# The scale of the first norm as one row, spread by TensorE into PSUM, with zero products on TensorE ahead of the first tile

## The chip, the cores and the metric

One core of a Trainium2 chip runs the whole program. The metric is device time in microseconds (us), the median of a few executions. The engines are TensorE (PE, with its weight loads PEld), VectorE (DVE), ScalarE (ACT), GpSimd (POOL) and SyncE (SP). Each has a queue of its own that it works in order; semaphores tie the queues together. Transfers are issued from SP's and POOL's queues.

## The reference, cut to what matters

Two transformer blocks of two layers each run one after the other on 256 tokens of width 1024, all in float32. The change touches the very first step alone, the norm in front of the first layer's input projection:

```python
def rms_norm(x, g):
    xf = x.astype(jnp.float32)
    y = xf * lax.rsqrt(jnp.mean(xf * xf, axis=-1, keepdims=True) + NORM_EPS)
    return (y * g.astype(jnp.float32)).astype(x.dtype)

for l in range(DEPTH):                       # DEPTH = 2
    h = rms_norm(x, mix_norm_g[l])           # x: (1, 256, 1024), g: (1024,)
    proj = h @ w_in[l]                       # and so on: attention, mlp
```

## The kernel before

The 256 tokens are two tiles of 128 (x, one token per partition, 1024 elements each). The norm of a tile runs over four engines. ScalarE squares and sums (`norm_root`, L756) and takes the root (L759). VectorE takes the reciprocal (L682) and multiplies x by it and by the scale g, in two halves of 512 columns, into `xs` (`norm_vector`, L687). TensorE transposes `xs` in eight pieces of 128 columns into PSUM (`turn_bank`, L818, with the identity `ident`). ScalarE copies the transposes to a rounded high part `xT` (L771), and VectorE makes the low part, the difference (L777).

Products are made of high and low parts of both operands, three products each of the rounded kind (`crossed`, L449). The weights come from memory in pieces of 128x1024 (512 KB) through a ring of seven slots, issued from SP's queue (L382). ScalarE rounds a piece to `w_high` (L403), VectorE makes `w_low` (L406). Each engine's order is written out by hand. On VectorE the low part of the first piece stands between the scaled tile and the low parts of `xT`, three more behind those, and only then the reciprocal of the second tile. The first matrix of products (`gemm_first`, key `swq`) works six of the eight row blocks of the first tile, with three products each, before the transposes of the second tile.

The scale g is a row of 1024 numbers in memory. Before the change POOL's first transfer (`opening`, L1182) writes it to all 128 partitions of a page in SBUF, the second brings the second tile of x. SP's queue issues the first tile of x (L1177), `ident` (L1178), then the pieces of weights. TensorE's program begins with one wait for `ident`:

```python
    @block.tensor
    def _(pe):
        pe.wait_ge(c.flag("ident_in").sem, 16)
```

VectorE waits for the scale (`gain_in`) in front of its first reciprocal, together with the wait for the root (`norm_std`).

Of the kernel before, what the change touches and what calls it, by code (L numbers as in the profile page):

```python
# [5 lines left out]
F32 = mybir.dt.float32  # L6
# [6 lines left out]
P = 128  # L13
# [3 lines left out]
D = 1024  # L17
# [5 lines left out]
HALF = 512  # L23
# [42 lines left out]
class Stream:  # L66
# [3 lines left out]
    def __init__(self):  # L70
        self.blocks, self.at = [], {}
        self.widths, self.split = [], []
# [205 lines left out]
class Core:  # L278


    def __init__(self, nc, ctx, counts):
        self.rotated = None
        self.roots_tried = 0
        self.nc, self.ctx, self.counts, self.flags = nc, ctx, counts, {}

        def sb(name, shape, dtype=F32):
            return ctx.enter_context(nc.sbuf_tensor(name, shape, dtype))

        self.sb = sb
        self.psum = ctx.enter_context(nc.psum_tensor("psum", [P, 8, HALF], F32))  # L290
        self.x = sb("x", [P, NT, D])
        self.xs = sb("xs", [P, NT, D])

        self.xT = sb("xT", [P, KD, 2, SEQ], F32R)
        self.xT_high, self.xT_low = self.xT[:, :, 0, :], self.xT[:, :, 1, :]
        self.w_high = sb("w_high", [P, SPLITS, PIECE], F32R)


        room = SEQ * 4 * 32 + PAGES * 4096 + SLOTS * PIECE * 4
        first = nc.sbuf_base + -nc.sbuf_base % 32  # L300
        sb("stretch", [P, room // 4 + 8])

        def placed(name, shape, dtype, offset):
            return nc.alloc_sbuf_tensor_at(name, shape, dtype, offset=first + offset)

        self.wide = placed("gates", [P, 32, SEQ], F32, 0)
        self.arena = placed("pages", [P, PAGES, 1024], F32, SEQ * 4 * 32)
        self.rounded = placed("rounded_pages", [P, PAGES, 1024], F32R, SEQ * 4 * 32)
        self.hidden = {
            KF1: [placed(f"hidden_1_{i}", [P, KF1, SEQ], F32R, i * KF1 * SEQ * 4) for i in range(2)],  # L310
            KF2: [placed(f"hidden_2_{i}", [P, KF2, SEQ], F32R, i * KF2 * SEQ * 4) for i in range(2)],
        }
        self.ring = placed("ring", [P, SLOTS, PIECE], F32, SEQ * 4 * 32 + PAGES * 4096)
        self.w_low = placed("w_low", [P, SLOTS, PIECE], F32R, SEQ * 4 * 32 + PAGES * 4096)
        self.attn_p = sb("attn_p", [P, 2, HALF])
        self.attn_pT = sb("attn_pT", [P, 2, HALF])
        self.ident = sb("ident", [P, P])
        self.tails = sb("tails", [P, 2, P])
        self.identb = sb("identb", [P, P], BF16)
        self.masks = sb("masks", [P, 4, HALF], BF16)  # L320
        self.rope = sb("rope", [P, NT, 4, HD])
        self.stats = sb("stats", [P, NT, 2, 6])
        self.mv = sb("mv", [P, NT, 2])
        self.rstd = sb("rstd", [P, NT, 2])
        self.mx = sb("mx", [P, NT, 8])
        self.nmx = sb("nmx", [P, NT, 8])
        self.rsum = sb("rsum", [P, NT, 8])
        self.all_heads_sums = sb("all_heads_sums", [P, NT, 8])
        self.fac = sb("fac", [P, NT, 8])


        self.rows_1 = sb("rows_1", [P, DEPTH, 2 * HD + 8])
        self.cols_2 = sb("cols_2", [P, 53 + 12 + 64])

        self.rope_cmp = self.page(9)[0:16, 896:1024].rearrange("p (x d) -> p x d", x=2)
        self.vcmp = self.page(9)[0:16, 768:896]
        self.cmp_valid = sb("cmp_valid", [P, NT])
        self.idle = sb("idle", [P, 3])
        self.eps = sb("eps", [P, 3])
        self.kcmp = sb("kcmp", [P, P])  # L340
        self.kcmpT = sb("kcmpT", [P, 32])
        self.head_rows = sb("head_rows", [P, 8 + P])
        self.branch_gates = sb("branch_gates", [P, NT, 24])
# [828 lines left out]
def opening(c, io, block):  # L1172


    @block.sync
    def _(sp):
        sp.dma_start(c.x[:, 0, :], io["x_in"][:, 0, :]).then_inc(c.flag("x_in0").sem, 16)  # L1177
        sp.dma_start(c.ident[:, :], io["ident"]).then_inc(c.flag("ident_in").sem, 16)  # L1178

    @block.gpsimd  # L1180
    def _(pool):
        pool.dma_start(c.page(16), io["gains_1"][0:1, :].to_broadcast([P, D])).then_inc(c.flag("gain_in").sem, 16)  # L1182
        pool.dma_start(c.x[:, 1, :], io["x_in"][:, 1, :]).then_inc(c.flag("x_in1").sem, 16)
        c.wait_landed(pool, 1)
        pool.dma_start(c.rows_1[:, :, :].rearrange("p l w -> p (l w)"),
                       io["rows_1"].rearrange("(o l) w -> o (l w)", o=1).to_broadcast([P, DEPTH * (2 * HD + 8)])
                       ).then_inc(c.flag("params_1").sem, 16)
        pool.dma_start(c.rope[:, :, :, :], io["rope"]).then_inc(c.flag("rope_in").sem, 16)
        pool.dma_start(c.tails[:, :, :], io["tails"]).then_inc(c.flag("tails_in").sem, 16)
        pool.dma_start(c.masks[:, :, :], io["masks"]).then_inc(c.flag("masks_in").sem, 16)  # L1190
        pool.dma_start(c.identb[:, :], io["ident"]).then_inc(c.flag("masks_in").sem, 16)
        pool.wait_ge(c.flag("idle_set").sem, 1)

    @block.vector
    def _(dve):
        dve.memset(c.idle[:, :], 0.0).then_inc(c.flag("idle_set").sem, 1)
        for i, eps in enumerate((RMS_EPS, LN_EPS, 4 * LN_EPS)):
            dve.memset(c.eps[:, i:i + 1], eps).then_inc(c.flag("eps_set").sem, 1)


def block_1(c, io, block, stream):
# [41 lines left out]
    gain = c.page(16)  # L1243
# [12 lines left out]
    def added(t, n):  # L1256
        _, b, use = banks.groups["down", t, n]
        return c.flag(f"drained{b}").at(DEPTH - 1, use + 1)

    @block.tensor  # L1260
    def _(pe):
# [15 lines left out]
        for l in c.layers(1):  # L1277
            def turn(j, t, l=l):
                return lambda h: c.norm_turn(pe, l, j, t, h, c.xs)

            if l == 0:
                for h in range(2):
                    turn(0, 0)(h)
            c.turn_later = turn(0, 1)
# [8 lines left out]
            def logits(h):  # L1293
                heads = [(c.psum[:, 4 + x % 2, :], slice(HD * (x % 2), HD * (x % 2 + 1)), x // 2) for x in (h, h + 1)]
                if h == 0:
                    if l == 0:
                        pe.wait_ge(c.flag("masks_in").sem, 32)
                        pe.wait_ge(c.flag("tails_in").sem, 16)
                    for key in ("sbq", "sbk"):
                        for n in range(2):  # L1300
                            c.wait_drained(pe, l, banks, (key, n))
                if h >= 2:
                    pe.wait_ge(*c.flag("sb_weighed").at(l, h))
                for z, _, _ in heads:
                    pe.matmul(z[:, 0:P], c.identb[:, :], c.masks[:, 3, 0:P], start=True, stop=False,
                              skip_group_check=True)
                    pe.matmul(z[:, SEQ:SEQ + P], c.identb[:, :], c.masks[:, 3, 0:P], start=False, stop=False,
                              skip_group_check=True)
                for z, r, k in heads:
                    pe.matmul(z[:, 0:SEQ], sbkT[r, k, 0:P], sbqT[r, k, :], start=False, stop=True,  # L1310
                              skip_group_check=True)
                for z, r, k in heads:
                    pe.matmul(z[:, SEQ:SEQ + P], sbkT[r, k, P:SEQ], sbqT[r, k, P:SEQ], start=False,
                              stop=True, skip_group_check=True).then_inc(*c.flag("sb_logits").one())
# [239 lines left out]
    def _(dve):  # L1554
# [6 lines left out]
        def add(key, layer, t, n):  # L1561
            half = c.x[:, t, n * HALF:(n + 1) * HALF]
            dve.tensor_tensor(half, half, c.filled(dve, layer, banks, (key, t, n)), ALU.add
                              ).then_inc(*c.drained(banks, (key, t, n)))
            c.wait_drained(dve, layer, banks, (key, t, n))

        for l in c.layers(1):
# [6 lines left out]
            def window_heads():  # L1574
# [20 lines left out]
                for i, (src, width, heads, ss, gain) in enumerate(((swq, 512, 8, c.rsum, 0), (swkv, P, 2, c.fac, HD))):  # L1595
# [10 lines left out]
                    for t in range(NT):  # L1606
# [2 lines left out]
                                 tmp[:, 2, 0:width], tmp[:, 3, 0:width], "roped" if t == NT - 1 else None)  # L1609
                        yield  # L1610

            c.norm_vector(dve, l, 0, c.x, c.xs,
                          first_rows if l == 0 else lambda t, n: add("down", l - 1, t, n), gain, None, split, -1,
                          lambda: dve.wait_ge(*c.flag("gain_in").at(l, 16)))
            side = window_heads()
            for key in ("swq", "swkv"):
                after(key)
# [1462 lines left out]
```

## Time and profile before

| | us |
|---|---|
| median of 3 runs | 2228.23 (2225.65 to 2231.48) |
| profiled execution | 2233.68 |
| its span in the profile | 2231.9 |
| TensorE busy | 2207.0 |
| VectorE busy | 1552.2 |
| ScalarE busy | 1110.0 |
| GpSimd busy | 198.4 |

The span is the part of the profiled execution that the trace covers, from the first instruction on. The times of the rows count from the span's start. A row of the timeline merges several instructions where they follow one another; "xcount" says how many. What stands in square brackets is the idle time of the engine in front of the row and what ended it.

### The profile page before, as it was taken

How to read it: one execution, taken by the hardware profiler on the slowest of the kernel's cores; microseconds unless marked ns; L12 is line 12 of the kernel's file. 1: busy time of each engine (PE TensorE's matmuls, PEld its weight loads, DVE VectorE, ACT ScalarE, POOL GpSimd, SP SyncE). 2: the span in 40 equal slices, each digit the busy share in tenths (PEclk: the TensorE clock that was granted, in tenths of full speed). 3: DMA queues.
4: the chain of work that ended last, by engine and by line, in shares of the span. 5: the costliest groups of instructions: out<-in, count | busy, mean ns of one | idle time of the engine just before them, and what ended most of it. 6: DMA issues, size and time to landing. Idle time of an engine off the chain costs nothing.

```text
span 2231.9 us, 34104 instructions
## 1 busy us (share of the span) xinstructions
PE 2207.0 (99%) x13650; PEld 1900.3 (85%) x13662; DVE 1552.2 (70%) x2163; ACT 1110.0 (50%) x1719; POOL 198.4 (9%) x191
## 2 busy tenths in 40 slices
PE   8999999999999999999999999999999999999998
PEld 7888888888888888888889988888888888998887
DVE  5777845677864775777787677567666777777764
ACT  4745434655543544445454554455444546355443
POOL 0010200001200110000004011011100000310110
PEclk9999999999999999999999999999999999999999
DMA  7445565445555755554535465565556444355553
GB/s 238 142 142 180 188 200 186 152 133 180 182 193 187 243 189 189 185 182 152 171 105 171 169 215 184 193 236 192 190 184 193 161 164 138 133 199 181 187 189 133
DMA packets 109245, 397.72 MB, mean 178 GB/s; under 512 B 12384, under 2 KB 12528, under 8 KB 108832
## 3 DMA queue, kind: packets, MB, share of 16 engines
q1 hardware_dynamic: 104256, 377.01, 50.8%
q0 software_dynamic: 4832, 18.53, 2.6%
q8 instruction: 109, 1.79, 0.3%
q14 instruction: 48, 0.39, 0.0%
HBM read 395.00 MB, written 1.05 MB: 177 GB/s over the span
## 4 chain that ended last, share of the span: by engine, by line
PE 96%; DVE 2%; ACT 1%; DMA 1%; issue 0%; DVEq 0%; SPq 0%; ACTq 0%; POOLq 0%
PE psum L449 44%; PE psum L600 29%; PE psum L599 15%; PE psum L818 2%; PE psum L963 2%; PE psum L940 1%; PE psum L927 1%; PE psum L898 1%; PE psum L2043 1%; PE psum L1319 0%; DMA ring<-in_weights 0%; DMA pages<-in_gains 0%; PE psum L1333 0%; ACT attn_p L1103 0%; DVE xs L2396 0%
## 5 line engine op out<-in xcount | busy, mean ns | idle before, releaser
L406 DVE TENSOR_TENSOR w_low<-ring,w_high 128x1024 fp32r<-128x1024 f32 x704 | 858.5, 1231 | 332.7 <-ACT w_high L403 331.3
L403 ACT ACTIVATE w_high<-ring 128x1024 fp32r<-128x1024 f32 x704 | 734.6, 1056 | 511.2 <-DMA ring<-in_weights 506.1
L600 PE MATMUL psum<-xT,w_high 128*128 128x512 f32 x2784 | 983.0, 397 | 0.0
L599 PE MATMUL psum<-xT,w_low 128*128 128x256 f32 x2784 | 790.3, 284 | 0.0
L600 PEld LDWEIGHTS psum<-xT,w_high 128*128 128x128 f32 x2784 | 522.8, 188 | 123.5 <-issue 1.0
L599 PEld LDWEIGHTS psum<-xT,w_low 128*128 128x128 f32 x2784 | 526.1, 189 | 3.9 <-issue 1.4
L449 PE MATMUL psum<-w_high,hidden 128*128 128x512 f32 x1216 | 376.9, 390 | 0.0
L449 PEld LDWEIGHTS psum<-w_high,hidden 128*128 128x128 f32 x1216 | 228.3, 188 | 47.2
L449 PE MATMUL psum<-w_low,hidden 128*128 128x512 f32 x608 | 236.6, 389 | 0.0
L449 PE MATMUL psum<-w_high,xT 128*128 128x512 f32 (+2 forms) x640 | 193.3, 382 | 0.7 <-DVE xT L777 0.6
L449 PE MATMUL psum<-rounded_pages,w_high 128*128 128x256 f32 x896 | 165.6, 286 | 0.0
L620 POOL TENSOR_TENSOR hidden<-attn_pT,hidden 128x256 fp32r<-128x256 f32 (+1 forms) x108 | 110.0, 1019 | 575.2 <-ACT hidden L2158 383.5
L449 PEld LDWEIGHTS psum<-rounded_pages,w_high 128*128 128x128 f32 x896 | 139.4, 191 | 1.8
L449 PEld LDWEIGHTS psum<-w_high,xT 128*128 128x128 f32 x640 | 118.3, 189 | 23.0 <-issue 2.0
L449 PEld LDWEIGHTS psum<-w_low,hidden 128*128 128x128 f32 x608 | 114.1, 188 | 23.7
L609 DVE TENSOR_REDUCE attn_p<-psum 128x256 f32<-128x512 f32 x136 | 93.8, 689 | 57.2 <-PE psum L600 57.0
L449 PE MATMUL psum<-rounded_pages,w_low 128*128 128x256 f32 x448 | 126.7, 283 | 0.0
L1103 ACT ACTIVATE attn_p<-psum,nmx 128x256 f32<-128x256 f32 (+2 forms) x176 | 67.9, 399 | 118.1 <-DVE nmx L1052 91.1
L449 PE MATMUL psum<-w_high,rounded_pages 128*128 128x512 f32 x384 | 123.7, 395 | 0.0
L449 PE MATMUL psum<-w_low,xT 128*128 128x512 f32 (+2 forms) x320 | 117.9, 379 | 0.0
L609 DVE TENSOR_REDUCE attn_pT<-psum 128x256 f32<-128x512 f32 x80 | 55.2, 690 | 63.8 <-PE psum L600 63.8
L2171 ACT ACTIVATE attn_p<-attn_p 128x256 f32<-128x256 f32 x80 | 33.4, 418 | 128.9 <-DVE attn_p L609 128.9
(238 smaller groups left out, 2089.0 us busy)
## 6 DMA issues: line engine op xcount, KB each, us to landing
ring<-in_weights SPq DMA_DIRECT2D x706, 512.0 KB, 3.5
pages<-in_affine POOLq DMA_DIRECT2D x16, 512.0 KB, 5.5
ring<-in_weights SPq DMA_DIRECT2D x8, 440.0 KB, 3.2
pages<-in_gains POOLq DMA_DIRECT2D x4, 512.0 KB, 4.8
pages<-in_mem POOLq DMA_DIRECT2D x2, 1024.0 KB, 6.6
pages<-in_bias POOLq DMA_DIRECT2D x2, 988.0 KB, 11.8
ring<-in_weights SPq DMA_DIRECT2D x4, 384.0 KB, 3.2
pages<-in_rows POOLq DMA_DIRECT2D x2, 512.0 KB, 5.8
```

Source lines behind the costliest of these rows:

```text
L403: eng.activation(high, raw, ACT.Copy).then_inc(self.flag("w_rounded").sem, 1)
L406: eng.tensor_tensor(self.w_low[:, piece % SLOTS, 0:width], raw, high.bitcast(F32), ALU.subtract).then_inc(self.flag("w_split").sem, 1)
L449: m = pe.matmul(out, a, b, start=(first and i == 0), stop=(last and i == len(pairs) - 1))
L599: pe.matmul(out[:, 0:SEQ], low, self.xT_high[:, k, :], start=(k == 0), stop=False, skip_group_check=True)
L600: m = pe.matmul(out, high, self.xT[:, k, :, :].rearrange("p x s -> p (x s)"), start=False, stop=(k == kn - 1), skip_group_check=True)
L609: dve.tensor_reduce(out, h.rearrange("p (x s) -> p s x", x=2), AX, ALU.add).then_inc(*self.drained(banks, key))
L620: pool.tensor_tensor(low, whole[:, n % (4 // tiles), :], high.bitcast(F32), ALU.subtract).then_inc(*self.flag("hidden").one())
L818: m = pe.transpose(out, src, self.ident[0:n, 0:n])
L898: m = pe.matmul(bank[:, i * w:(i + 1) * w], q, k, start=not started, stop=True, skip_group_check=True)
L963: m = pe.matmul(self.psum[rows, 7, h * dv:(h + 1) * dv], self.attn_pT[0:n, u % 2, c * P + rows.start:c * P + rows.stop], a["v"](h, kt), st ...
L1103: m = act.activation(self.attn_p[:, u % 2, i * w:(i + 1) * w], self.psum[:, 4 + u % 2, i * w:(i + 1) * w], ACT.Exp, bias=self.nmx[:, t, h: ...
L2171: act.activation(silu[:, n % 4, :], silu[:, n % 4, :], ACT.Silu).then_inc(*c.flag("silu").one())
```

## The change

The scale's transfer brings one row of 4 KB to one partition instead of 128 copies. VectorE first fills 512 columns of `xT` with zeros and a row `ones` with ones. TensorE multiplies the zeros five times (512 columns each, rounded kind), then waits for the row and multiplies `ones` by it, once for each half, in plain float32, so that PSUM banks 2 and 3 hold the scale on all 128 partitions; then it multiplies zeros four times more. VectorE reads the scale of the first layer's first norm from those banks, for both tiles; its first reciprocal waits for the two spreading products. All other norms stay as they were. The wait for `ident` stays at the head of TensorE's program.

```diff
+        self.ones = sb("ones", [1, P])
...
     @block.gpsimd
     def _(pool):
-        pool.dma_start(c.page(16), io["gains_1"][0:1, :].to_broadcast([P, D])).then_inc(c.flag("gain_in").sem, 16)
+        pool.dma_start(c.page(16)[0:1, :], io["gains_1"][0:1, :]).then_inc(c.flag("gain_in").sem, 16)
         pool.dma_start(c.x[:, 1, :], io["x_in"][:, 1, :]).then_inc(c.flag("x_in1").sem, 16)
...
     @block.vector
     def _(dve):
+        dve.memset(c.xT[:, 0, :, :].bitcast(F32), 0.0).then_inc(c.flag("warm_set").sem, 1)
+        dve.memset(c.ones[:, :], 1.0).then_inc(c.flag("ones_set").sem, 1)
         dve.memset(c.idle[:, :], 0.0).then_inc(c.flag("idle_set").sem, 1)
...
             if l == 0:
+                idle_columns = c.xT[:, 0, :, :].rearrange("p x s -> p (x s)")
+
+                def warm(n):
+                    for _ in range(n):
+                        pe.matmul(c.psum[:, 0, :], idle_columns[:, 0:P], idle_columns, start=True, stop=True)
+
+                pe.wait_ge(c.flag("warm_set").sem, 1)
+                warm(5)
+                pe.wait_ge(c.flag("ones_set").sem, 1)
+                pe.wait_ge(*c.flag("gain_in").at(l, 16))
+                for n in range(2):
+                    pe.matmul(c.psum[:, 2 + n, :], c.ones[:, :], gain[0:1, n * HALF:(n + 1) * HALF], start=True, stop=True
+                              ).then_inc(c.flag("gain_spread").sem, 1)
+                warm(4)
                 for h in range(2):
                     turn(0, 0)(h)
...
-            c.norm_vector(dve, l, 0, c.x, c.xs,
-                          first_rows if l == 0 else lambda t, n: add("down", l - 1, t, n), gain, None, split, -1,
-                          lambda: dve.wait_ge(*c.flag("gain_in").at(l, 16)))
+            if l == 0:
+                c.norm_vector(dve, l, 0, c.x, c.xs, first_rows, c.psum[:, 2:4, :].rearrange("p n w -> p (n w)"), None,
+                              split, -1, lambda: dve.wait_ge(c.flag("gain_spread").sem, 2))
+            else:
+                c.norm_vector(dve, l, 0, c.x, c.xs, lambda t, n: add("down", l - 1, t, n), gain, None, split, -1,
+                              lambda: dve.wait_ge(*c.flag("gain_in").at(l, 16)))
```

The head of TensorE's order before (the names in brackets are the flags that a row waits for; `xn_ready` is a finished half of `xs`):

```order
L1260 UNCONDITIONAL_BRANCH [waits barrier_Pool_Activation_PE_DVE_SP_release]
L818 MATMUL psum<-ident,xs 128x128 [waits xn_ready,ident_in]
L818 MATMUL psum<-ident,xs 128x128 x3
L818 MATMUL psum<-ident,xs 128x128 [waits xn_ready]
L818 MATMUL psum<-ident,xs 128x128 x3
L449 MATMUL psum<-w_high,xT 128x512 [waits w_split,turned_dve,drained0]
```

And in the changed kernel, where line numbers are shifted (L819 is the old L818; `pages,ones` is the spreading of the scale):

```order
L1263 UNCONDITIONAL_BRANCH [waits barrier_Pool_Activation_PE_DVE_SP_release]
L1289 MATMUL psum<-xT 128x512 [waits warm_set,ident_in]
L1289 MATMUL psum<-xT 128x512 x4
L1296 MATMUL psum<-pages,ones 128x512 [waits gain_in,ones_set]
L1296 MATMUL psum<-pages,ones 128x512
L1289 MATMUL psum<-xT 128x512 x4
L819 MATMUL psum<-ident,xs 128x128 [waits xn_ready]
```

Eleven products stand ahead of the first transpose, and the wait for `ident` moved from the transpose to the first of them.

The head of VectorE's order before, from its first instruction to the second half of `xs`:

```order
L1196 MEMSET idle 128x3
L1198 MEMSET eps 128x1 x3
L1553 UNCONDITIONAL_BRANCH
L682 RECIPROCAL rstd<-rstd 128x1 [waits norm_std,gain_in,x_in0]
L687 SCALAR_TENSOR_TENSOR xs<-x,rstd,pages 128x512 [waits dve_step]
L687 SCALAR_TENSOR_TENSOR xs<-x,rstd,pages 128x512
```

And in the changed kernel:

```order
L1197 MEMSET xT 128x512
L1198 MEMSET ones 1x128
L1199 MEMSET idle 128x3
L1201 MEMSET eps 128x1 x3
L1570 UNCONDITIONAL_BRANCH
L683 RECIPROCAL rstd<-rstd 128x1 [waits norm_std,gain_spread,x_in0]
L688 SCALAR_TENSOR_TENSOR xs<-x,rstd,psum 128x512 [waits dve_step]
```

Two fills are put in front, and the reciprocal waits for TensorE's `gain_spread` where it waited for the transfer `gain_in`.

## Rows read from the trace of the kernel before

**Rows 1.** The page's head: the span, and each engine's busy time.
```profile
span 2231.9 us, 34104 instructions
PE 2207.0 (99%) x13650; PEld 1900.3 (85%) x13662; DVE 1552.2 (70%) x2163; ACT 1110.0 (50%) x1719; POOL 198.4 (9%) x191
```

**Rows 2.** Busy time by stretch: length, PE, PEld, DVE, ACT, POOL, PEclk, DMA share, GB/s.
```profile
0.00:20.00 20.00, 9.91 (x40) 8.05 (x41) 9.78 (x17) 10.27 (x16) 4.11 (x11) 1.00 0.89 311
20.00:500.00 480.00, 479.56 (x3148) 414.92 (x3153) 330.08 (x457) 250.33 (x372) 27.03 (x21) 1.00 0.52 168
```

**Rows 3.** TensorE's waits: who for whom, us in total, times, longest.
```profile
PE psum L818 <- DVE xs L687: 9.5, 1, 9.5
```

**Rows 4.** Timeline to 12 us: start, length, engine, line, operation.
```profile
1.24 0.42 SPq L1178 DMA_DIRECT2D ident<-in_ident  x1
1.32 0.69 POOL L1182 DMA_DIRECT2D pages<-in_gains  x1 [0.81 <-POOLq L3071]
...
6.41 0.29 ACT L759 ACTIVATE rstd<-mv,eps 128x1 f32<-128x1 f32 x1
8.38 0.16 DVE L682 RECIPROCAL rstd<-rstd 128x1 f32<-128x1 f32 x1 [7.36 <-DMA pages<-in_gains]
8.58 1.41 DVE L687 SCALAR_TENSOR_TENSOR xs<-x,rstd,pages 128x512 f32<-128x512 f32 x2
...
9.48 1.94 PE L818 MATMUL psum<-ident,xs 128*128 128x128 f32 x8 [9.48 <-DVE xs L687]
9.91 1.22 DVE L406 TENSOR_TENSOR w_low<-ring,w_high 128x1024 fp32r<-128x1024 f32 x1
...
11.23 0.69 DVE L777 TENSOR_TENSOR xT<-psum,xT 128x512 fp32r<-128x512 f32 x1
```

**Rows 5.** Transfers: count, KB, median us from issue to landing (last: whole program).
```profile
pages<-in_gains POOLq DMA_DIRECT2D x1, 512.0 KB, 7.0
...
ident<-in_ident SPq DMA_DIRECT2D x1, 64.0 KB, 4.1
identb<-in_ident POOLq DMA_DIRECT2D x1, 32.0 KB, 9.0
...
ring<-in_weights SPq DMA_DIRECT2D x706, 512.0 KB, 3.5
```

**Rows 6.** Timeline of TensorE, 12 to 20 us.
```profile
12.03 0.76 PE L449 MATMUL psum<-w_high,xT 128*128 128x512 f32 x1 [0.60 <-DVE xT L777]
12.59 0.63 PE L449 MATMUL psum<-w_low,xT 128*128 128x512 f32 x1
13.02 1.05 PE L449 MATMUL psum<-w_high,xT 128*128 128x512 f32 x2
...
15.15 0.53 PE L449 MATMUL psum<-w_low,xT 128*128 128x512 f32 x1
15.52 0.62 PE L449 MATMUL psum<-w_high,xT 128*128 128x512 f32 x2
15.97 0.40 PE L449 MATMUL psum<-w_low,xT 128*128 128x512 f32 x1
...
18.27 0.60 PE L818 MATMUL psum<-ident,xs 128*128 128x128 f32 x4
```

**Rows 7.** Timeline of TensorE near 69 us: plain float32 products, two records each.
```profile
69.44 0.81 PE L1319 MATMUL psum<-pages,tails 128*128 128x384 f32 x2
70.08 0.38 PE L1321 MATMUL psum<-pages,tails 128*128 128x128 f32 x2
```

**Rows 8.** Timeline of VectorE, 13 to 17 us.
```profile
13.03 3.50 DVE L406 TENSOR_TENSOR w_low<-ring,w_high 128x1024 fp32r<-128x1024 f32 x3 [0.18 <-ACT w_high L403]
16.64 0.17 DVE L682 RECIPROCAL rstd<-rstd 128x1 f32<-128x1 f32 x1
```

**Rows 9.** VectorE by line and form: count, busy us, mean ns, idle before.
```profile
L2396 DVE SCALAR_TENSOR_TENSOR xs<-x,psum 128x512 f32<-128x512 f32 x32 | 21.9, 683 | 14.7 <-PE psum L449 14.2
L687 DVE SCALAR_TENSOR_TENSOR xs<-x,rstd,pages 128x512 f32<-128x512 f32 x16 | 11.3, 749 | 0.3
```

## The prediction

> **What bounds the kernel now.** I read the first lines of the page first. TensorE is busy for 2207.0 of 2231.9 us [rows 1], so all its idle time together is 24.9 us, and a change that leaves TensorE's own work alone can give back no more than a part of that. The view of busy time by stretch says where the idle time lies: TensorE works 9.91 of the first 20 us, so 10.1 us are lost there, and from 20 to 500 us it loses 0.44 us [rows 2]. The view of waits names the largest one: 9.5 us, once, for the first scaled tile `xs` of VectorE [rows 3]. The change sits in exactly this stretch. Behind it TensorE runs without a gap, so whatever moment it reaches its steady stream is carried unchanged to the end: a microsecond lost or won at the start is a microsecond of the total, and nothing multiplies it. That alone limits the effect to a few tenths of a per cent.
>
> The timeline of the first 13 us gives the chain [rows 4]. ScalarE has the root of the mean of squares done at 6.41 + 0.29 = 6.70. VectorE starts its reciprocal only at 8.38: it waits for the scale `gains`, issued at 1.32 and 7.0 us in flight [rows 4, 5], so it landed at 8.32. From 8.38 (call this moment T0) VectorE works without a gap: the reciprocal and two halves of `xs`, then the first low weight part from 9.91, then at 11.23 the first `xT` part, 0.69 long; TensorE's first product follows at 12.03, that is T0 + 3.65.
>
> The rows of TensorE after that show its clock [rows 6]. Products of 512 columns start 0.43 us apart (12.59 to 13.02), and after 15.52 they start 0.23 apart (15.52 to 15.97, two of them): 512 columns in 0.43 are 1.2 GHz, in 0.23 nearly 2.4 GHz. (The column of the granted clock says 1.00 for the whole stretch [rows 2], so the level is read from the starts.) The rise lies between 15.15 and 15.52, say 15.3: 5.8 us after TensorE's first work (the transposes at 9.48), 3.3 us after the first 512-column product.
>
> **The change part by part.** *What it hopes to remove* is the gap from 6.70 to 8.38 on VectorE, 1.7 us, and the slow products after 12.03. But VectorE now waits for TensorE, and TensorE's queue is in order: in the order of TensorE the five zero products stand ahead of the two spreading ones, and the first of the five carries the wait for `ident`, which used to stand at the first transpose and was covered by the wait for `xs`. `ident` is issued at 1.24 and is 4.1 us in flight [rows 4, 5]: it lands at 5.34. The gains took 0.06 from landing to the reciprocal, so TensorE starts at 5.40, not near 1.
>
> *Five zero products* at the slow 0.43: 2.15, to 7.55.
>
> *The two spreading products* are plain float32, not the rounded kind of the weight products. A float32 product of 384 columns is two records, and the pair takes 70.08 - 69.44 = 0.64 us at the full clock [rows 7]: 0.32 per 384 columns, twice the time per column of a 512-column weight product. For 512 columns that is 0.64 x 512/384 = 0.85 per product, 1.71 for both at the full clock and 3.41 at the half one. That only one of 128 rows is filled takes nothing off in this sum: no row shows that fewer rows are quicker.
>
> *When does the clock rise?* Counted from the first 512-column product as before, at 5.40 + 3.3 = 8.7; counted from the first work, at 5.40 + 5.8 = 11.2. TensorE's first work is now a run of 512-column products, so I take the row that is nearest, 3.3 us. Then the spreading runs slow from 7.55 to 8.7, 1.15 of 3.41 or 34%, and the other 66% of 1.71 take 1.13: 9.83. With 0.2 for the last product's way out and the signal (the pair of 384 columns lasts 0.81 where its successor starts after 0.64 [rows 7]), the reciprocal starts at 10.0: T0 moves by +1.6. With the late rise: 7.55 + 3.41 + 0.2 = 11.2, +2.8.
>
> *What comes back behind T0.* The four later zero products fit between the spreading and the first transpose, which comes 1.1 us after T0 as before (9.48 - 8.38): four take 0.92 at the full clock. To the first `xT` part nothing changes, since VectorE is busy all the way. From then on both engines gain. The second half's transposes take half the time (four of them last 0.60 us at 18.27 against 1.94 for eight at 9.48), so the next high parts and the three low parts, which VectorE works from 13.03 to 16.53 [rows 8], each about 0.4 to 0.5 us sooner after T0. TensorE's eight slow products, 0.2 too long each, cost 1.6 us; at full speed six products of one piece of weights take 1.38 and VectorE delivers a low part every 1.17, so TensorE has to wait some 0.5 for the second piece. What is left is about 1.0 us: the transposes of the second tile, at 18.27 or T0 + 9.9 before, come at about T0 + 8.9, behind a second reciprocal at T0 + 7.8 instead of T0 + 8.26.
>
> *The small parts.* Filling 512 columns of `xT` with zeros is not in the trace; at most 0.75 us by VectorE's operations of that width, and more than nothing ([rows 9] has 0.683 and 0.749 with two inputs, this has none). It ends before 2 us, while TensorE waits for `ident` until 5.34, and the `eps` filled behind it are needed for the root at 6.41: covered, and without the cover at most 0.75. The scale as a PSUM operand: an operation of the same kind and width with a PSUM input takes 0.683 against 0.749 with all in SBUF [rows 9], so four of them win 0.26 at most, of which one or two lie on the chain: -0.1, which I leave in the bounds. The Trainium skill ("VectorE: DVE Perf Modes", section on the TRN2 errata) has a fixed part of 58 cycles for SBUF to SBUF and of 120 for PSUM to SBUF; by it each would take 0.06 longer and the sum would be +0.1, an estimate; the trace's rows say the opposite, and the sum goes by them.
>
> *The row's landing.* POOL's queue issues 4 KB where it issued 512 KB. TensorE needs it at 7.55. Bounds: it lands no later than the 512 KB did, 8.32, if it is like its predecessor; the trace has also a 32 KB transfer of the same queue that took 9.0 us (`identb`, behind 512 KB of masks [rows 5]), which would be 10.3. At the other end, the 512 KB pieces of weights take 3.5 us at the median [rows 5]: 4.8. It is the first transfer of its queue, as the gains were, and those had 128 times as much to move, so I take a landing before 7.55 and no wait. The Trainium skill ("DMA: Bandwidth & Descriptors", Anatomy of one DMA) gives a transfer from this queue about 2 us and its bytes over 436 GB/s: by that it lands near 3.4, an estimate, and the sum is the same; `identb`'s 9.0 us show that this trace does not bear the rule out under load. The 508 KB that no longer flow make the second tile of x and the weights land earlier; ScalarE and VectorE reach them later than before, so nothing comes of it.
>
> *Sum*: +1.6 for T0, -1.0 behind it: +0.6 us. In the profiled execution's own time that is 2233.68 + 0.6; that execution lies above all three timed runs (2225.65 to 2231.48), so I carry the difference to their median: 2228.23 + 0.6 = 2228.8 us.
>
> **The rivals.** *The spread is early, faster.* With less traffic beside it `ident` may land after 3.5 us as a piece of weights does: 4.74. If the clock were full from the start, TensorE would run 1.15 + 1.71 from 4.8, and T0 would be 7.9: -0.5, and with the 1.0 behind it -1.5: 2226.7. For it: the gains' half megabyte was in flight at the same time as x and `ident`. Against: the second tile of x follows on the same queue at once, and no row shows TensorE at full clock in its first 3 us.
>
> *Half clock throughout.* If the zeros and the thin products do not raise the clock, T0 is 11.2, the four later zeros end 0.6 after the transposes could start, and nothing comes back: +3.4, 2231.6. Against: the rise before came within 5.8 us of any work. If it only comes at 11.2, the rest is at full clock and the sum is +2.8 - 1.0 = +1.8, 2230.0.
>
> *Slower: the row is late and blocks TensorE.* The second wait of TensorE stands in front of the spreading, the later zeros and all transposes, so nothing passes it. It decides from a landing after 7.55. With `identb`'s 9.0 us: 10.3, then the spreading slow again after 2.8 us of idleness, 13.7, T0 = 13.9, +5.5, and less than 1.0 back: about +5, 2233. To be slower by 0.3% (6.7 us) the row would have to land after 11 us.
>
> *The change does nothing to T0*: the spreading happens to end at 8.2. This needs `ident` 1.6 us earlier than before; -1.0, 2227.2. It lies inside the first rival.
>
> **How the numbers follow.** Forecast, a spread between 9.4 and 11.2 and a sum from 0 to +1.8: 0.70. Early spread: 0.12. Half clock throughout: 0.08. Late row: 0.07. Something outside these: 0.03. No case but the last and the tail of the late row leaves the 0.3% (6.7 us, about what a measurement of this kernel can tell from no change): faster 0.02, same 0.95, slower 0.03. The range joins the mechanisms' -1.5 to +3.4 with the scatter of a few runs (the three lie 5.8 us apart): 2225.4 to 2232.8.
>
> **What would show it.** In the profile after: TensorE's first work at about 5.4, not at 1 to 2; five products 0.43 apart; four float32 records whose spacing falls from 0.85 to 0.43; the reciprocal at about 10.0, released by TensorE and not by a transfer; TensorE's first weight product 3.6 after it and from there 0.23 apart with a wait for a low part after the sixth; transposes of the second tile near 18.9. TensorE's busy time grows, and its idle time falls by about as much, with the span unmoved. I am wrong if the reciprocal starts before 8.4, if TensorE waits for the row after the fifth zero product, or if any difference arises behind 20 us.

## The result, and the profile after

The changed kernel takes 2231.26 us (median of 20 runs, 2230.05 to 2233.91); beside it the kernel before took 2226.72 (20 runs). The ratio is 1.0018, 95% interval 1.0012 to 1.0025, so the change costs 2.7 to 5.6 us. The forecast was +0.6: 2228.8 for a median of 2228.23. It stays within the 0.3% (6.7 us) that the prediction named, and it is slower by more than the measurement's scatter.

The page's head of the changed kernel: TensorE is busy for 2.6 us more than in [rows 1], with its extra products.

```profile
span 2229.6 us, 34145 instructions
PE 2209.6 (99%) x13675; PEld 1900.8 (85%) x13675; DVE 1551.1 (70%) x2165; ACT 1108.8 (50%) x1719; POOL 199.2 (9%) x191
```

(The spans of the two profiled executions, 2231.9 and 2229.6, are one execution each and lie the other way round than the medians: the one of before was above every one of its first three timed runs. What is compared below is the start, stage by stage, and the times of many runs.)

The timeline of TensorE in the changed kernel, for [rows 4, 6]: start, length, operation, count, and the wait in front.

```profile
5.67 2.50 PE L1289 MATMUL psum<-xT 128*128 128x512 f32 x5 [5.67 <-DMA ident<-in_ident]
8.10 3.78 PE L1296 MATMUL psum<-pages,ones 1*128 1x512 f32 x4
11.81 2.08 PE L1289 MATMUL psum<-xT 128*128 128x512 f32 x4
13.68 1.56 PE L819 MATMUL psum<-ident,xs 128*128 128x128 f32 x8
16.20 0.47 PE L450 MATMUL psum<-w_high,xT 128*128 128x512 f32 x1 [0.95 <-issue]
16.50 0.40 PE L450 MATMUL psum<-w_low,xT 128*128 128x512 f32 x1
16.74 0.63 PE L450 MATMUL psum<-w_high,xT 128*128 128x512 f32 x2
...
18.14 0.50 PE L450 MATMUL psum<-w_high,xT 128*128 128x512 f32 x1 [0.31 <-DVE w_low L407]
...
22.82 0.47 PE L450 MATMUL psum<-w_high,xT 128*128 128x512 f32 x1
```

The reader is to see three things. TensorE starts only when `ident` lands. The four records of the spreading take 3.7 us, from 8.10 to 11.81, 0.93 each in the mean, and the four zero products behind them are still slow: 1.87 us to 13.68, 0.47 each. And from 16.20 on the weight products run at the full rate (16.50 to 16.74). The last row is the first product behind both turns of the second tile; I call it the stream's start, since TensorE is busy without a gap from there. It stood at 19.64 before, so the start is 3.18 us later:

```profile
19.64 0.47 PE L449 MATMUL psum<-w_high,xT 128*128 128x512 f32 x1
```

The timeline of VectorE there, for [rows 4, 8]:

```profile
0.98 0.48 DVE L1197 MEMSET xT<- 128x512 f32 x1 [0.98 <-PEq L3091]
...
11.98 0.16 DVE L683 RECIPROCAL rstd<-rstd 128x1 f32<-128x1 f32 x1 [10.35 <-PE psum L1296]
...
15.40 1.29 DVE L778 TENSOR_TENSOR xT<-psum,xT 128x512 fp32r<-128x512 f32 x2 [0.69 <-ACT xT L772]
```

The reciprocal comes at 11.98 instead of 8.38, released by TensorE. VectorE then waits 0.69 us for the high part, since the transposes began 1.70 after the reciprocal instead of 1.10: the slow zeros stood in front of them.

The transfers, for [rows 5]:

```profile
ident<-in_ident SPq DMA_DIRECT2D x1, 64.0 KB, 4.4
...
pages<-in_gains POOLq DMA_DIRECT2D x1, 4.0 KB, 4.5
```

The row lands at 1.32 + 4.5 = 5.8, long before TensorE asks for it.

### The profile page after: what moved, and what is told of

The parts are those of the page before. It is cut to its first block, busy times and chain, and to the rows that moved or that the text cites. A ratio compares the mean times of both kernels' runs of the same rounds, so it can differ in the third digit from the quotient of the medians.

```text
span 2229.6 us, 34145 instructions
## 1 busy us (share of the span) xinstructions
PE 2209.6 (99%) x13675; PEld 1900.8 (85%) x13675; DVE 1551.1 (70%) x2165; ACT 1108.8 (50%) x1719; POOL 199.2 (9%) x191
## 4 chain that ended last, share of the span: by engine, by line
PE 96%; DVE 2%; ACT 1%; issue 0%; DMA 0%; DVEq 0%; SPq 0%; ACTq 0%
PE psum L450 43%; PE psum L601 28%; PE psum L600 15%; PE psum L819 2%; PE psum L964 2%; PE psum L941 1%; PE psum L899 1%; PE psum L928 1%; PE psum L2063 1%; PE psum L1336 0%; DVE w_low L407 0%; ACT attn_p L1104 0%; ACT psum L753 0%; PE psum L1350 0%; DVE x L688 0%
```

## The experiments

The theory after the result (A): products of zeros do raise TensorE's clock, but in the changed kernel the run of spreading products, one row high, keeps it at the half level, 1.2 GHz; so spreading and later zeros are slow, and everything hangs on them. The rivals: zeros don't raise it at all (B); or the rise was late by chance (C). "Stream" is the first product behind the second tile's turns, as above; 19.64 before, 22.82 in the change.

| run | reciprocal | stream | ratio to before, 95% |
|---|---|---|---|
| the change | 11.98 | 22.82 | 1.0018 (1.0012 to 1.0025) |
| e8, the change again | 11.86 | 23.08 | 1.0022 (1.0014 to 1.0031) |
| e1, zeros alone | 8.03 | 19.71 | 1.0000 (0.9992 to 1.0009) |
| e2, no zeros | 9.79 | 21.59 | 1.0009 (1.0000 to 1.0018) |
| e3, ident later | 9.69 | 20.86 | 1.0011 (1.0002 to 1.0020) |
| e4, rounded spread | 9.38 | 21.84 | 1.0012 (1.0004 to 1.0021) |
| e5, x behind the scale | 8.00 | 24.87 | 1.0024 (1.0014 to 1.0035) |
| e6, zeros to the products | 7.88 | 23.68 | 1.0018 (1.0010 to 1.0027) |
| e7, full rows, zeros | 7.46 | 20.66 | one run, 2227.93 us |
| e12, one row, zeros | 7.32 | 23.61 | 1.0024 (1.0015 to 1.0034) |
| e10, spread in full rows | 12.56 | 22.47 | 1.0012 (1.0003 to 1.0020) |
| e9, halves and early | 7.20 | 22.28 | 1.0004 (0.9996 to 1.0013) |
| e11, halves, plain order | 7.05 | 18.11 | 1.0003 (0.9992 to 1.0013) |

Reciprocal and stream are read from one profiled execution of each kernel. In all twelve rows with an interval the shift of the stream against 19.64 lies within the interval of the time (the change: 3.18 in 2.7 to 5.6; e9: 2.64 in -0.9 to +2.9). That agrees with a start that is carried to the end; the intervals, some 3 to 5 us wide, prove no more.

### Zeros alone

```diff
-pool.dma_start(c.page(16)[0:1, :], io["gains_1"][0:1, :])       # against the change
+pool.dma_start(c.page(16), io["gains_1"][0:1, :].to_broadcast([P, D]))
...
-pe.matmul(c.psum[:, 2 + n, :], c.ones[:, :], gain[0:1, ...])    # and VectorE waits for gain_in again
-warm(4)
+warm(3)
```

> The scale comes by the old transfer of 512 KB and VectorE waits for that; only the zero products (eight, behind the wait for ident) are left of the change. Theory A (zero products raise TensorE's clock; what kept it at the half level for 9 us in the changed kernel is the run of one-row float32 products between them): the reciprocal stays at 8.4, the starts of the products fall from 0.43 to 0.23 us apart between 8.5 and 9.5, the first weight products run at the full rate, and the steady stream behind the second tile's transposes begins about 1.0 us earlier than before (19.64): ratio 0.9995. Theory B (products of zeros don't raise the clock, whatever stands between them): weight products 0.43 apart until about 15 as before, stream at 19.6, ratio 1.000.

TensorE in this run:

```profile
5.34 3.54 PE L1289 MATMUL psum<-xT 128*128 128x512 f32 x8 [5.34 <-DMA ident<-in_ident]
...
8.48 0.40 PE L1289 MATMUL psum<-xT 128*128 128x512 f32 x1
9.03 1.32 PE L819 MATMUL psum<-ident,xs 128*128 128x128 f32 x8 [0.15 <-DVE xs L688]
12.32 0.76 PE L450 MATMUL psum<-w_high,xT 128*128 128x512 f32 x1 [1.97 <-DVE xT L778]
12.88 0.63 PE L450 MATMUL psum<-w_low,xT 128*128 128x512 f32 x1
```

The last zero product lasts 0.40 where the slow ones of [rows 6] last 0.63, and the eight transposes take 1.32 where they took 1.94: zeros raised the clock, 3.1 us after they began. B falls. But TensorE then stood for 1.97 us until the first weight product, and that started slow again, 0.43 apart. So the zeros gave nothing back here, neither in the stream nor in the time. The expected -1.0 missed: A had the rise right and forgot the gap behind the transposes.

### No zeros; ident later; the change again

```diff
-pe.wait_ge(c.flag("warm_set").sem, 1)      # e2: and no fill of xT
-warm(5)
...
-warm(4)
```

> The change without any zero product and without their fill: the spreading products follow the landing of ident and of the row. Both theories: spreading from about 5.9 (row 5.8, ident 5.7), four records 0.93 apart, the reciprocal at 9.8 instead of 11.98, transposes not held up; the clock rises only behind the first weight products at 13.4, so near 16.5; stream at 21.0, +1.4 us against before and 1.8 to 3 less than the change: ratio 1.0006. A third theory C (any work raises the clock, it was only late by chance): spacing of the four records falls before the last, reciprocal at 9.0, stream at about 19.0, ratio 0.9998.

```diff
 def _(pe):                                  # e3
-    pe.wait_ge(c.flag("ident_in").sem, 16)
...
     warm(4)
+    pe.wait_ge(c.flag("ident_in").sem, 16)
     for h in range(2):
         turn(0, 0)(h)
```

> The change with the wait for ident moved from the head of TensorE's program to the first transpose. Five zero products from 1.6 to 3.8, then TensorE idle until the row lands at 5.8, spreading to 9.6, reciprocal at 9.8 (2.2 earlier than in the change), four zero products to 11.4. Theory A: the zeros from 9.6 on raise the clock at 12 to 13, during or just behind the transposes, stream at 20.3, +0.6 against before. Theory B: the transposes wait for slow zeros until 11.4, the first weight products come at 13.9 and are slow until 15 or later; stream at 21.3, +1.6.

> The changed kernel once more, for a second look at when its clock rises. Theory A (the one-row products don't raise it): spreading records 0.93 apart all four, reciprocal near 12.0, rise at 13 to 16. If the late rise was chance: rise between 8.5 and 11, reciprocal at 10 to 11. Ratio 1.001 to 1.002 by theory A.

Without zeros the reciprocal was at 9.79, as expected, and the stream at 21.59, 0.6 later than expected: the clock rose only at 18.1, not near 16.5.

```profile
5.94 3.75 PE L1293 MATMUL psum<-pages,ones 1*128 1x512 f32 x4 [5.94 <-DMA pages<-in_gains]
```

The spreading begins at 5.94 there and at 8.10 in the change: the five zeros in front cost it 2.2 us, and that is the difference of the reciprocals. In the run with `ident` later TensorE shows:

```profile
5.84 3.75 PE L1295 MATMUL psum<-pages,ones 1*128 1x512 f32 x4 [1.82 <-DMA pages<-in_gains]
9.52 2.08 PE L1288 MATMUL psum<-xT 128*128 128x512 f32 x4
11.39 1.88 PE L819 MATMUL psum<-ident,xs 128*128 128x128 f32 x8
13.90 0.47 PE L450 MATMUL psum<-w_high,xT 128*128 128x512 f32 x1 [0.64 <-issue]
```

Zeros and transposes behind the spreading are slow, the weight products at 13.90 fast: the rise comes after 12.5, more than 3 us after the last zeros began. The stream, 20.86, lies between A's 20.3 and B's 21.3. The second profile of the change (e8) gave nearly the first one's numbers: four records in 3.71, reciprocal 11.86, all eight transposes slow until 15.3, where in the first the clock rose within them, at 14.6. C has no support.

### Is it float32, the single row, or its data?

```diff
-self.ones = sb("ones", [1, P])              # e4
+self.ones = sb("ones", [1, P], F32R)
...
-pool.dma_start(c.page(16)[0:1, :], io["gains_1"][0:1, :])
+pool.dma_start(c.rounded[0:1, 16, :], io["gains_1"][0:1, :])
```

> The change with the row and the ones of the rounded kind of the weight products, so that each spreading product is one record instead of two slower ones; the row is rounded by its transfer, so the scale loses its last digits. Order and zeros as in the change. Both theories: spreading in 0.86 instead of 3.7 us, reciprocal at 9.2. Theory A: clock full by about 9.5, stream at 19.4, -0.2 against before. If it is the single row of data and not the float32 kind that fails to raise the clock, 10 to 12 and stream at 19.9. Theory B: later zeros to 10.7 hold the transposes by 0.4, weight products slow until 14 to 16, stream at 20.9, +1.2.

```diff
-pe.matmul(c.psum[:, 2 + n, :], c.ones[:, :], gain[0:1, n * HALF:(n + 1) * HALF], start=True, stop=True
+pe.matmul(c.psum[:, 2 + n, :], idle_columns[:, 0:P].bitcast(F32), idle_columns.bitcast(F32), start=True,      # e7
+pe.matmul(c.psum[:, 2 + n, :], idle_columns[0:1, 0:P].bitcast(F32), idle_columns[0:1, :].bitcast(F32), ...    # e12
```

> The changed kernel's order of products, with the two spreading products replaced by two float32 products of the same columns whose 128 rows are all filled (zeros by zeros); the scale comes by the old transfer. If it is the single filled row that left the clock at the half level: full rate 3 to 4 us after the first zero product, so at 8.5 to 9.5, spacing of the float32 records from 0.85 to 0.43, all zeros done by 11.0. If float32 products of any height do it: records 0.85 to 0.93 apart to the end, zeros 0.43 apart until after 13, as in the changed kernel.

> The twin of e7_full_rows: the same order and the same transfer of the scale, the two float32 products of zeros one row high instead of 128. Nothing else differs, the data neither. In e7_full_rows the four zero products behind them ran at the full rate, 0.23 apart from 11.3 on, 5.9 us after the first zero product. If the single row is what kept the clock down in the changed kernel: the four float32 records 0.93 apart, the four zeros behind them 0.43 to 0.47 apart, rise 2.8 to 4.5 us after these began, so at 14 to 16. If it was the data of the row, or chance: zeros 0.23 apart from about 11.5 on as in the twin.

Rounded products of one row, e4:

```profile
8.07 1.22 PE L1296 MATMUL psum<-rounded_pages,ones 1*128 1x512 f32 x2
9.22 2.08 PE L1289 MATMUL psum<-xT 128*128 128x512 f32 x4
...
18.01 0.53 PE L450 MATMUL psum<-w_low,xT 128*128 128x512 f32 x1
```

The spreading shrinks to 1.15 us and the reciprocal to 9.38, but the clock stays half until 18.1, so a late rise does not need the float32 kind. (e4 leaves out the exactness of the scale: its output is a tenth off, and it stands for its timing alone.) By itself e4 does not show that the single row is the cause: its products ahead of the transposes cover 5.5 us (5.64 to 11.09), and in e6, further down, zeros of 128 rows alone took 5.6 us to raise the clock. The twins e7 and e12 differ by the height of two products of zeros alone. TensorE with 128 rows, and then with one:

```profile
7.65 3.59 PE L1294 MATMUL psum<-xT 128*128 128x512 f32 x4
8.50 1.06 PE L1294 MATMUL psum<-xT 128*128 128x512 f32 x1
...
11.31 0.62 PE L1289 MATMUL psum<-xT 128*128 128x512 f32 x2
11.54 0.62 PE L1289 MATMUL psum<-xT 128*128 128x512 f32 x2
...
11.99 1.04 PE L819 MATMUL psum<-ident,xs 128*128 128x128 f32 x8
14.05 0.47 PE L450 MATMUL psum<-w_high,xT 128*128 128x512 f32 x1 [1.02 <-issue]
```

```profile
7.67 3.78 PE L1294 MATMUL psum<-xT 1*128 1x512 f32 x4
11.38 2.08 PE L1289 MATMUL psum<-xT 128*128 128x512 f32 x4
13.25 1.91 PE L819 MATMUL psum<-ident,xs 128*128 128x128 f32 x8
...
19.32 0.78 PE L450 MATMUL psum<-w_high,xT 128*128 128x512 f32 x2
```

(The row at 8.50 is one of the four records above it, the rows at 11.31 and 11.54 share a record: they come from narrow windows.) With 128 rows the zeros behind start 0.23 apart (11.31 to 11.54), the transposes take 1.04, and the stream begins at 20.66. With one row the zeros take 0.47 each, the transposes 1.91, and the full rate comes only after 19.3; the stream begins at 23.61, 2.95 us later, and the time is that of the change. The data are the same, so for what stands behind the two products it is the single row. One profile stands for each twin, but others agree: with one-row products in between, 8.0 us of work up to the transposes did not raise the clock in e12 (5.24 to 13.25), in the change or in e8, while with 128 rows and no wait in between the rise came within 5.7 us in every run with zeros. Two sizes missed: even with 128 rows the four float32 records stayed slow (7.65 to 8.50 is 0.85, as between one-row records), so the rise came only near 11, 5.7 us after the first zero product, against 3.1 in the run with zeros alone; and with one row it came not at 14 to 16 but past 19.3. So the single row does not explain why the spreading itself is slow in the change; it explains that the clock is still half behind it.

### The spreading in full rows

```diff
-self.ones = sb("ones", [1, P])
+self.ones = sb("ones", [P, P])              # ones in row 0, zeros below; page 16 filled with zeros first
...
-... gain[0:1, n * HALF:(n + 1) * HALF], start=True, stop=True
+... gain[:, n * HALF:(n + 1) * HALF], start=True, stop=True
```

> The changed kernel with the spreading products made 128 rows high: ones is a 128x128 tile with ones in its first row and zeros below, and the page that takes the row is filled with zeros first, so that the same scale comes out. The row's transfer waits for the fills, issued near 2.8, landing near 7.2, still ahead of the fifth zero. If the one filled row is what kept the clock down: rise 3 to 4 us after the first zero at 5.6, so at 8.6 to 9.6, spread by 10.0 to 10.7, reciprocal at 10.2 to 10.9 instead of 11.9, later zeros at the full rate, stream at 20.5 to 21.2 against 22.8 to 23.1 of the change. If not: reciprocal at 11.9 and stream at 22.9.

```profile
8.88 3.58 PE L1301 MATMUL psum<-pages,ones 128*128 128x512 f32 x4 [0.74 <-DMA pages<-in_gains]
...
12.53 0.63 PE L1293 MATMUL psum<-xT 128*128 128x512 f32 x2
12.77 0.63 PE L1293 MATMUL psum<-xT 128*128 128x512 f32 x2
```

The row landed at 8.8 and not at 7.2, so TensorE waited and the reciprocal came later, at 12.56, against the expected 10.2 to 10.9. The clock behaves as in e7: the spreading is slow with full rows too, 3.68 us from its start to the reciprocal against 3.88 in the change, so the expected rise within it did not come. The zeros behind it start 0.24 apart (12.53 to 12.77) where they start 0.43 or more apart in the change. The stream, 22.47, misses the expected 20.5 to 21.2 but gains 0.35 on the change in spite of the later reciprocal: it comes 9.91 us behind it, against 10.84 in the change.

### Can a version beat both?

```diff
 pool.dma_start(c.page(16), io["gains_1"][0:1, :].to_broadcast([P, D])).then_inc(...)
+pool.wait_ge(c.flag("gain_in").sem, 16)     # e5, and e6 with zeros from 1.5 us and behind the transposes
 pool.dma_start(c.x[:, 1, :], io["x_in"][:, 1, :]).then_inc(...)
```

> The kernel before with one wait more: POOL issues the second tile of x only when the 512 KB of the scale have landed. No zeros, no spreading. If the scale's 7.0 us come from sharing its queue with the second tile of x: landing near 6.5, reciprocal at 6.9 instead of 8.4, first weight product at 10.6, stream at 18.3, -1.3 us: ratio 0.9994. If the weights' pieces are what it shares with: landing and reciprocal stay at 8.0 to 8.4, ratio 1.000; and if the first piece of weights then lands late the low part of it holds VectorE, 1.000 too. The slower end: the second tile of x comes after 15 and its sum of squares is late, +0.5.

> The run before this one (e5_x_behind_scale), with zero products around the first transposes: eighteen from 1.5 us on, ahead of the wait for ident, and five more between the transposes and the first weight product (zeros in a slot of w_high that is written later). Theory A: clock full by 5 to 6, kept to the first weight product, which starts at 10.6 and runs 0.23 apart at once; stream at 17.3, 1.0 before the run without zeros: ratio 0.999. If the clock falls in the gaps that stay: as the run without zeros, or up to 0.5 later because the last five zeros are slow.

Without the second tile of x behind it the scale landed 6.6 us after its issue. With the tile behind it it took 7.0 (before), 6.6 (e1), 6.1 (e7) and 5.9 (e12), so no gain from the wait is shown. And the tile then came too late, by the row of VectorE in e5:

```profile
15.63 0.69 DVE L777 TENSOR_TENSOR xT<-psum,xT 128x512 fp32r<-128x512 f32 x1 [4.09 <-DMA x<-in_x_in]
```

VectorE stands for 4.09 us at a wait for the second tile that lies in front of the first tile's second half: 5.2 us for the stream, 3.1 to 7.8 in time. e6 falls with it, though its zeros kept the clock up to the first weight products: transposes in 1.23, first weight products 0.23 apart. The rise came later than the hoped 5 to 6; TensorE in e6, with two of the eighteen zeros alone:

```profile
1.52 6.90 PE L1289 MATMUL psum<-w_high 128*128 128x512 f32 x18 [1.52 <-DVE w_high L1198]
6.38 0.63 PE L1289 MATMUL psum<-w_high 128*128 128x512 f32 x1
7.12 0.40 PE L1289 MATMUL psum<-w_high 128*128 128x512 f32 x1
```

```diff
-lambda: dve.wait_ge(c.flag("gain_spread").sem, 2))                    # e9, e11: first half waits for 1, second for 2
+lambda: dve.wait_ge(c.flag("gain_spread").sem, 1), half_way=half_way)
...
-warm(5)                                     # zeros in a slot of w_high, from 1.5 us, ident waited for later
+warm(10)
...
-warm(4)
+warm(2)                                     # and behind them the wait for ident
...
+                warm(3)                     # behind the transposes; 6 in e11
```

> The row spread as in the change, with three edits: zeros start at 1.5 (ident waited for only at the first transpose, ten products, in a slot of w_high that is written later), VectorE waits for each half of the spread scale on its own with the first low weight part between them, and three more zeros stand between the transposes and the first weight product. By the theory that zeros raise the clock and one-row products don't: clock full somewhere between 4.6 and 7 us. If it is full when the row lands at 5.8: first half spread by 6.9, reciprocal at 7.1, first weight product at 10.8, stream at 18.0, -1.6 against before: ratio 0.9993. If it is still at the half level there: first half by 7.9, second by 9.8, first weight product near 11.6, stream at 19.0 to 19.3, -0.4 to -0.6. Rival: the row or the order of VectorE costs more than that (low weight part waits for its piece), +0.5.

> The run e9_halves_and_early with VectorE's old order restored (the first low weight part behind both halves of the scaled tile, each half waiting for its own spreading product) and six instead of three zeros between the transposes and the first weight product. What the earlier runs say adds up to: clock full before 5, spreading from 5.9 in 1.9 to 2.0, reciprocal at 7.2, second half done by 8.9; then the first low weight part waits for the first piece of weights, which ScalarE took up at 6.9 to 9.4 in the other runs. Taken up at 7: first weight product at 11.0, at the full rate, stream at 18.1, -1.5. Taken up at 9.4: first weight product at 12.6, stream at 19.7, 0. So between ratio 0.9993 and 1.000; the theory that it is the single filled row that keeps the clock down would be wrong if the rate fell back within the spreading.

In both the zeros from 1.5 us had raised the clock before the row landed, and the spreading ran at the full rate. TensorE in e9, then TensorE and VectorE in e11:

```profile
5.98 1.95 PE L1297 MATMUL psum<-pages,ones 1*128 1x512 f32 x4 [0.48 <-DMA pages<-in_gains]
7.86 1.12 PE L1290 MATMUL psum<-w_high 128*128 128x512 f32 x2
8.78 1.05 PE L821 MATMUL psum<-ident,xs 128*128 128x128 f32 x4
```

```profile
5.83 1.98 PE L1297 MATMUL psum<-pages,ones 1*128 1x512 f32 x4
...
9.37 2.91 PE L1290 MATMUL psum<-w_high 128*128 128x512 f32 x6
12.07 0.50 PE L450 MATMUL psum<-w_high,xT 128*128 128x512 f32 x1
...
18.11 0.47 PE L450 MATMUL psum<-w_high,xT 128*128 128x512 f32 x1
```

```profile
7.05 0.16 DVE L683 RECIPROCAL rstd<-rstd 128x1 f32<-128x1 f32 x1 [5.42 <-PE psum L1297]
```

Four records in 1.98 us, the reciprocal at 7.05, 1.3 before that of the kernel before, and a stream at 18.11, 1.5 earlier. But the clock fell again behind the one-row products: in e9 at once, where the next two zeros took 0.92 (7.86 to 8.78), and in e11 by 9.37 (six zeros in 2.70). TensorE had been idle for no more than 0.48 us there, while idle gaps of 0.95 us in the change and 1.02 in e7 left the full rate as it was. So 1.9 us of one-row products did more harm than those gaps, a second sign that it is the single row; what part the transposes have in e11 is not separated. In e9 the first piece of weights was late, and its low part, which my order had put between the halves, held the second half until 11.63: stream at 22.28. In time neither differs from before, 1.0004 and 1.0003. Whether e11 is worth its 1.5 us could not be told: its interval reaches from -1.8 to +2.9 us. No version was shown to beat the kernel before.

## Why the prediction was right or wrong

*Where the path leads*: right. The first wait for `ident` (now at 5.67), VectorE's wait for TensorE and a later reciprocal are all there, and the stream starts 3.18 us later, inside the measured 2.7 to 5.6. The medians differ by 4.5; whether the last 1.3 are more than scatter stays open. The two profiled executions can't tell it: the changed one's span is 2.3 shorter, so they differ by 5.5 us the other way behind the start.

*T0*: the step that failed is "When does the clock rise?". I took 3.3 us after the first product, in the middle of the spreading. The reciprocal came at 11.98, not 10.0. Of the 2.0 us, 0.27 are `ident` (landing 4.4 us after issue, not 4.1), 0.28 the five zeros (2.43, not 2.15), and 1.43 the spreading and its end (3.88, not 2.45), which stayed at the half clock to the end. The 3.3 was one reading from one execution. With 128 rows throughout, the runs gave 3.1 (e1) to 5.7 us (e7), and in e7 and e10 the four records of full rows stayed slow too (in e10 3.68 us to the reciprocal, not 3.88), so of the 1.43 only some 0.2 can be put down to the single row; what sets the moment of the rise is open. My late bound, 5.8, fits e7 and should have stood in the forecast's middle and not at its edge.

*What comes back*: predicted 1.0, measured 0.42 (the stream at T0 + 10.84 against T0 + 11.26). Here the single row tells, which I had dismissed with "no row shows that fewer rows are quicker"; the question should have been what else it might change. The clock was still half behind the spreading: the later zeros took 1.87, not 0.92, and held the transposes by 0.6 and the first weight product by 0.57 (T0 + 4.22). With full rows in e10 the stream came at T0 + 9.91. The weight products at the full rate then gave back about 1.0, as worked out, with the wait for the second low part (0.31).

*The rivals*: "half clock throughout" had 0.08 and comes nearest, with its T0 of 11.2 and 2231.6 us, but partly by luck. T0 came 0.8 later still: the late `ident`, the 0.28 of the five zeros and 0.27 of the spreading. And "nothing comes back" was wrong: the clock rose at 14.6, and zeros do raise it (e1). By its own figures its later zeros would have held the transposes by 0.4, not 0.6. My forecast's own range, 0 to +1.8, was too narrow. That 2231.26 lies within the stated 2225.4 to 2232.8 is owed to this rival and to the scatter joined to the range, and to a base that stood 1.5 above the 20 runs' 2226.72; it is no merit of the forecast. The late row did not occur (5.8 against 7.55).

*Small parts*: the fill took 0.48 and was covered. The PSUM operand gave nothing, by the view of VectorE by line and form in the changed kernel (the first row has the scale in SBUF, in other norms, the last has it in PSUM):

```profile
L688 DVE SCALAR_TENSOR_TENSOR xs<-x,rstd,pages 128x512 f32<-128x512 f32 x12 | 8.5, 749 | 0.2
...
L688 DVE SCALAR_TENSOR_TENSOR xs<-x,rstd,psum 128x512 f32<-128x512 f32 x4 | 2.8, 745 | 0.1
```

745 against 749 ns: neither my -0.066 each from [rows 9], whose 683 belong to another line with fewer operands, nor the +0.06 of the table that I cited from the Trainium skill ("VectorE: DVE Perf Modes", section on the TRN2 errata). For the landing of the row the rule that I cited from the Trainium skill ("DMA: Bandwidth & Descriptors", Anatomy of one DMA) gave some 2 us, an estimate; it was 4.5 in a queue with nothing in front.

## What to carry to other kernels

Before a wait is moved onto another engine, read what stands ahead of the new releaser in that engine's queue: here a wait for an unrelated transfer and 2.4 us of filler, and the filler in front of a needed result cost 2.2 us of its 2.4 (e2). A rate is read from rows of the same shape as the new work, its height included, and the moment of a clock's rise from more than one execution; where they are missing, both levels belong in the likeliest case's own range. No filler here was shown to be worth its time. In e1 its rate was lost in 1.97 us without work, while 0.95 to 1.02 us did no harm (the change, e7); and between a result and the one who waits for it, filler put the stream's start off (22.82 in the change against 21.59 without zeros).

## What the runs showed that was not expected

- Products one row high left TensorE at the half level: with them in between, the full rate came 8.9 us (the change), over 9.7 (e8), 12.5 (e4) and over 14 us (e12) after the first zero product; with 128 rows throughout, 3.1 (e1), about 5.7 (e7) and, for zeros from 1.5 us on, about 3 to 4 (e9, e11) and 5.6 (e6, from eighteen of them in 6.90 us). In e10, with a wait of 0.74 us in between, it was there by 6.9. What sets the spread within each kind is not settled.
- A float32 record of one row and 512 columns is not slower in itself. Single records of the spreading in the changed kernel, from narrow windows:

```profile
9.12 1.06 PE L1296 MATMUL psum<-pages,ones 1*128 1x512 f32 x1
9.97 1.06 PE L1296 MATMUL psum<-pages,ones 1*128 1x512 f32 x1
10.82 1.06 PE L1296 MATMUL psum<-pages,ones 1*128 1x512 f32 x1
```

They start 0.85 apart, as records of 128 rows do in e7. The first takes 1.02 (8.10 to 9.12) and the last 0.99 (10.82 to 11.81): the extra stands at the two ends of the run, where the height changes, and makes the mean of 0.93.
- With the scale as 4 KB instead of 512 KB, the first tile of x and `ident` landed later, not earlier: `ident` 4.3 to 4.4 us after issue in eight runs, against 3.9 to 4.1 in the six with 512 KB. The second tile of x, next on the scale's own queue, landed earlier, 7.3 to 7.9 us after issue against 8.2 to 9.6 in the four with 512 KB just ahead of it. Why is open.
- The first piece of weights, issued at the same moment in every kernel, was taken up by ScalarE anywhere from 6.9 to 9.4 us.
